# 8x8 diagonal blocks inverted by forward substitution on VectorE in a hybrid decoder trunk

## What is computed

```
    m = jnp.where(strict, jnp.einsum('nbhcd,nbhsd->nbhcs', k_beta, k) * decay, 0.0)
    eye = jnp.eye(c, dtype=m.dtype)
    t_inv = lax.linalg.triangular_solve(eye + m, jnp.broadcast_to(eye, m.shape),
                                        left_side=True, lower=True)
    u = t_inv @ v_beta
    w = t_inv @ (k_beta * jnp.exp(gc)[..., None])
```

## Time and profile before

| | |
|---|---|
| time, median of 3 runs | 2122.13 us (2121.14 to 2122.16) |
| the profiled execution | 2121.77 us, its span 2119.9 us |
| TensorE (PE) busy | 2046.7 us, 97% of the span |
| VectorE (DVE) busy | 1084.8 us, 51% |
| ScalarE (ACT) busy | 756.4 us, 36% |
| GpSimd (POOL) busy | 737.0 us, 35% |
| mean granted TensorE clock | 0.99 |

### The profile page before, as it was taken

How to read it: one execution, slowest core, us unless ns; L and a number is a source line. 1 busy time by engine, 2 the same in 40 slices (tenths; PEclk the granted TensorE clock), 3 DMA queues, 4 the chain that set the end, 5 groups by cost and what they waited for, 6 DMA issues and landing times.

```text
span 2119.9 us, 34678 instructions
## 1 busy us (share of the span) xinstructions
PE 2046.7 (97%) x14608; PEld 1574.7 (74%) x14608; DVE 1084.8 (51%) x1782; ACT 756.4 (36%) x1180; POOL 737.0 (35%) x550
## 2 busy tenths in 40 slices
PE   5999999999999999999989999999999999999997
PEld 4788787756667888888867877876566678888886
DVE  6694654796843422222367844458967343222223
ACT  4541613344353432322253243133443434332322
POOL 2430303331313444444435122133222344444442
PEclk8999999999999999999999999999999999999998
DMA  5320111221322323333332111122113223232331
GB/s 188 102 81 15 48 32 61 92 85 38 114 61 70 115 93 99 91 98 96 93 110 86 47 36 56 33 74 95 50 40 125 65 80 100 90 99 95 95 96 63
DMA packets 52266, 170.04 MB, mean 80 GB/s; under 512 B 5648, under 2 KB 13968, under 8 KB 51600
## 3 DMA queue, kind: packets, MB, share of 16 engines
q1 hardware_dynamic: 50928, 162.75, 24.1%
q0 software_dynamic: 1184, 5.07, 0.6%
HBM read 160.45 MB, written 7.34 MB: 79 GB/s over the span
## 4 chain that ended last, share of the span: by engine, by line
PE 84%; DVE 11%; ACT 3%; issue 1%; DMA 1%; SPq 0%; DVEq 0%; ACTq 0%
PE bank_a L467 13%; PE bank_a L468 12%; PE bank_a L471 12%; PE bank_v L471 7%; PE bank_v L467 7%; PE bank_v L468 7%; PE bank_v L609 5%; PE bank_v L531 4%; DVE mg L1425 1%; DVE arena L1419 1%; PE bank_a L739 1%; PE bank_f L563 1%; PE bank_f L569 1%; PE bank_f L542 1%; PE bank_a L728 1%
## 5 line engine op out<-in xcount | busy, mean ns | idle before, releaser
L428 POOL TENSOR_TENSOR w_lo<-ring,w_hi 128x512 fp32r<-128x512 f32 x536 | 730.6, 1384 | 1263.2 <-ACT w_hi L1107 1263.1
L467 PE MATMUL bank_a<-h_hi,w_hi 128*128 128x512 f32 x1312 | 531.0, 405 | 6.7 <-ACT w_hi L1107 6.7
L468 PE MATMUL bank_a<-h_lo,w_hi 128*128 128x512 f32 x1312 | 512.7, 391 | 0.0
L1107 ACT ACTIVATE w_hi<-ring 128x1024 fp32r<-128x1024 f32 x268 | 281.6, 1051 | 222.4 <-DVE arena L1951 220.1
L471 PE MATMUL bank_a<-h_hi,w_lo 128*128 128x512 f32 x1312 | 324.1, 389 | 0.0
L467 PEld LDWEIGHTS bank_a<-h_hi,w_hi 128*128 128x128 f32 x1312 | 247.2, 188 | 77.7 <-issue 19.4
L468 PEld LDWEIGHTS bank_a<-h_lo,w_hi 128*128 128x128 f32 x1312 | 247.3, 188 | 58.3 <-issue 8.1
L471 PEld LDWEIGHTS bank_a<-h_hi,w_lo 128*128 128x128 f32 x1312 | 246.3, 188 | 51.2
L467 PE MATMUL bank_v<-parts,w_hi 128*128 128x512 f32 x640 | 254.5, 398 | 1.4 <-DVE parts L1922 1.4
L468 PE MATMUL bank_v<-parts,w_hi 128*128 128x512 f32 x640 | 253.4, 396 | 0.0
L1419 DVE TENSOR_TENSOR sg<-bank_v,sg 128x512 f32<-128x512 f32 x112 | 77.5, 692 | 327.3 <-PE bank_v L471 256.3
(11 more groups left out here) (281 smaller groups left out, 2430.2 us busy)
## 6 DMA issues: line engine op xcount, KB each, us to landing
ring<-in_w SPq DMA_DIRECT2D x268, 512.0 KB, 3.5
out_ring<-in_w SPq DMA_DIRECT2D x64, 128.0 KB, 3.5
x_dram<-arena SPq DMA_DIRECT2D x2, 2048.0 KB, 8.9
arena<-x_dram SPq DMA_DIRECT2D x2, 2048.0 KB, 9.8
arena<-in_x SPq DMA_DIRECT2D x2, 1024.0 KB, 8.1
arena<-tabs POOLq DMA_DIRECT2D x4, 512.0 KB, 4.5
out_x<-arena SPq DMA_DIRECT2D x2, 1024.0 KB, 4.3
par<-in_par POOLq DMA_DIRECT2D x2, 937.0 KB, 7.1
```

The source lines that it names most:

```text
L428: ins = nc.gpsimd.tensor_tensor(w_lo[:, g % SPLIT, ks, :], raw, w_hi[:, g % SPLIT, ks, :].bitcast(F32), ALU.subtract)
L467: mm(b[:], w_hi[:, s, k, :], hi[:, k, :], start=k == 0, stop=False)
L468: mm(b[:], w_hi[:, s, k, :], lo[:, k, :], start=False, stop=False)
L1107: act_fn(w_hi[:, g % SPLIT, :, :], ring[:, g % RING, :, :], ACT.Copy).then_inc(S["split_hi"], 1)
```

## The change

The three smallest block sizes are taken out of the doubling: `first_steps` (block size 2) and the levels 2 and 4 go, and the 8x8 diagonal blocks are inverted directly.

- `block_columns` on VectorE: `u` is multiplied by a mask of the 8x8 blocks (128x1024), and a reduction over the block index packs the eight columns of each row's block into a compact tile `uc` of 128x128 (16 pairs by 8).
- `spread_rows` on TensorE: seven matmuls against 0/1 matrices `row0` to `row6` (128x128, in `consts`) copy row k of each block to all eight rows of the block, for columns k+1 to 7. They go into one bank of `bank_v`, in the middle of the gate product (after its 16 matmuls with `w_hi`, ahead of the 8 with `w_lo`).
- `block_inverses` on VectorE: a copy of the identity, and for k = 0 to 6 a product of the spread row with column k of the inverse, and a subtraction from the later columns. Every operation waits for the one before. Two operations of 128x512 put the compact inverse back into the 64x64 layout.
- `block_columns` stands between `masked` for `u` and the next `masked`; `block_inverses` stands where `first_steps` stood.
- `consts` loses four tiles of 64 columns and gains one of 64, one of 8 and seven of 128.

```diff
-LEVELS = (2, 4, 8, 16, 32)
+LEVELS = (8, 16, 32)
+BLOCK = 8
...
-    parts.append(("first_c", half(-1.0 * level(1).T)))
+    parts.append(("blocks_c", half(i // BLOCK == j // BLOCK)))
+    parts.append(("eye_b", (i % BLOCK == j)[:, :BLOCK]))
+    for k in range(BLOCK - 1):
+        parts.append((f"row{k}", i == j // BLOCK * BLOCK + k))
...
-        ("eye_c", half(np.eye(P))),
...
-            def split_product(g, b, hi, lo, sem_name=None, k0=0):
+            def split_product(g, b, hi, lo, sem_name=None, k0=0, between=None):
...
+                if between:
+                    between()
                 pe.wait_ge(S["split_lo"], g + 1)
...
+            def spread_rows(l, x, V):
+
+                b, reader, emptied = banks.next("v", x + "_e")
+                pe.wait_ge(reader, emptied)
+                pe.wait_ge(S[x + "_uc"], at(l, x + "_uc", 1))
+                uc, at_ = compact(V, 0), 0
+                for k in range(BLOCK - 1):
+                    n = M * (BLOCK - 1 - k)
+                    ins = mm(b[:, at_:at_ + n], cst(f"row{k}"), uc[:, :, k + 1:BLOCK], start=True, stop=True)
+                    at_ += n
+                ins.then_inc(v_full, 1)
...
-                numbers = [gate(l, 2, 0)]
+                numbers = [gate(l, 2, 0, lambda: spread_rows(l, "r", R))]
...
-                numbers.append(gate(l, 2, 7))
+                numbers.append(gate(l, 2, 7, lambda: spread_rows(l, "g", G)))
...
-            def first_steps(x, V):
+            def block_columns(x, V):
+
+                tt(V["x"], V["u"], cst("blocks_c").unsqueeze(1).to_broadcast([P, M, C]), MUL)
+                v.tensor_reduce(compact(V, 0), V["x"].rearrange("p m (b j) -> p m j b", j=BLOCK), AX_X, ADD).then_inc(S[x + "_uc"], 1)
+
+            def block_inverses(x, V):
+
+                xc = compact(V, 1)
+                link(v.tensor_copy(xc, cst("eye_b").unsqueeze(1).to_broadcast([P, M, BLOCK])))
+                dve.wait_ge(v_full, filled.next())
+                b, at_ = filled.bank(), 0
+                for k in range(BLOCK - 1):
+                    n = BLOCK - 1 - k
+                    product = compact(V, 2)[:, :, 0:n]
+                    ins = v.tensor_tensor(product, b[:, at_:at_ + M * n].rearrange("p (m c) -> p m c", c=n),
+                                          xc[:, :, k:k + 1].to_broadcast([P, M, n]), MUL)
+                    if k == BLOCK - 2:
+                        ins.then_inc(S[x + "_e"], 1)
+                        dve.wait_ge(S[x + "_e"], reached(x + "_e"))
+                    else:
+                        link(ins)
+                    tt(xc[:, :, k + 1:BLOCK], xc[:, :, k + 1:BLOCK], product, SUB)
+                    at_ += M * n
                 for half in range(2):
                     ms = slice(half * M // 2, (half + 1) * M // 2)
-                    tt(V["x"][:, ms, :], V["u"][:, ms, :], wide("first_c"), MUL)
-                    v.tensor_tensor(V["x"][:, ms, :], V["x"][:, ms, :], wide("eye_c"), ADD).then_inc(S[x + "_x1"], 1)
+                    shape = [P, M // 2, C // BLOCK, BLOCK]
+                    v.tensor_tensor(V["x"][:, ms, :].rearrange("p m (b j) -> p m b j", j=BLOCK), xc[:, ms, :].unsqueeze(2).to_broadcast(shape),
+                                    cst("blocks_c").rearrange("p (b j) -> p b j", j=BLOCK).unsqueeze(1).to_broadcast(shape), MUL).then_inc(S[x + "_x1"], 1)
...
                 masked("r", R["u"], lambda hp: wide("before_c"))
                 dve.wait_ge(S["r_tok"], at(l, "r_tok", 8))
+                block_columns("r", R)
                 masked("r", R["akk"], lambda hp: wide("before_c"))
-                first_steps("r", R)
+                block_inverses("r", R)
                 masked("r", R["ark"], lambda hp: wide("upto_c"))
                 masked("r", R["arb"], lambda hp: wide("upto_c"))
...
                 masked("g", G["u"], lambda hp: of_parity(G["d"], hp))
+                block_columns("g", G)
                 masked("g", G["arb"], lambda hp: of_parity(G["d"], hp))
-                first_steps("g", G)
+                block_inverses("g", G)
```

More of the change, by code:

```diff
@@ L41 @@
 RW_ORDER = (6, 7, 2, 3, 0, 1, 4, 5)
-LEVELS = (2, 4, 8, 16, 32)
-INVERSE_STEPS = ("x1", "ti", "y", "t", "x", "wt", "u")
+LEVELS = (8, 16, 32)
+BLOCK = 8
+INVERSE_STEPS = ("uc", "e", "x1", "ti", "y", "t", "x", "wt", "u")
 GDN0, MLA0, RWK0, DSA0, GATE0 = 0, 1032, 1448, 2472, 3824
@@ L260, in build @@
             ("r_ex", 1), ("r_sq", 1), ("r_l2", 2), ("r_l2s", 1), ("r_bsq", 2), ("r_bon", 2), ("r_feat", 4),
-            ("r_tok", 8), ("r_mat", 8), ("r_x1", 2), ("r_ti", 2), ("r_y", 10), ("r_t", 8), ("r_x", 10),
+            ("r_tok", 8), ("r_mat", 8), ("r_uc", 1), ("r_e", 1), ("r_x1", 2), ("r_ti", 2), ("r_y", 6), ("r_t", 4), ("r_x", 6),
             ("r_wt", 2), ("r_y1", 2), ("r_u", 2), ("r_ws", 2 * NC), ("r_s", NC), ("r_o", NC),
@@ L266, in build @@
             ("g_row", 2), ("g_d", 2), ("g_prep", 1),
-            ("g_tok", 6), ("g_mat", 4), ("g_x1", 2), ("g_ti", 2), ("g_y", 10), ("g_t", 8), ("g_x", 10),
+            ("g_tok", 6), ("g_mat", 4), ("g_uc", 1), ("g_e", 1), ("g_x1", 2), ("g_ti", 2), ("g_y", 6), ("g_t", 4), ("g_x", 6),
             ("g_wt", 2), ("g_u", 2), ("g_ws", 2 * NC), ("g_s", NC), ("g_o", NC),
@@ L317, in bank, with compact @@
                 return self.banks[(self.n - 1) % len(self.banks)]
+        def compact(V, i):
+            n = M * BLOCK
+            return V["y"].rearrange("p m c -> p (m c)")[:, i * n:(i + 1) * n].rearrange("p (m c) -> p m c", c=BLOCK)
         def of_parity(view, hp):
@@ L504, in token_root, with gate @@
                 ins.then_inc(v_full, 1)
-            def gate(l, br, m):
+            def gate(l, br, m, between=None):
                 g = begin_unit(("merge", br, m), l)
@@ L510, in gate @@
                 pe.wait_ge(reader, emptied)
-                split_product(g, b, h_hi, h_lo).then_inc(a_full, 1)
+                split_product(g, b, h_hi, h_lo, between=between).then_inc(a_full, 1)
                 return merges_to(g)
```

## The result

The changed kernel takes 2084.73 us (median of 4 runs, 2081.71 to 2086.87) where the kernel before takes 2122.05 beside it: a ratio of 0.9823, 95% interval [0.9808, 0.9838].

A forecast was written before the change was run, and what follows sets the result against it. TensorE, busy 97% of the span, was taken as the bound, with VectorE late ahead of RWKV's levels. 2 x (6.2 - 11.35 + 1.6 - 11.44) + 1.0 = -29.0 us gave 2093, range 2085 to 2102.

The forecast's parts named there:

- Levels: Two full levels go from each inversion: 11.35 us of TensorE in RWKV, 11.44 in GDN, all on the path.
- RWKV delay: The first `y` left in the RWKV branch comes 6.2 us later, VectorE being late; bounds 3.5 to 9.3.
- The chain: Seven dependent products and seven subtractions on VectorE in `block_inverses`: 3.64 us with gaps.
- the spreading: Seven matmuls on TensorE that spread the rows, 0.23 us each whatever the width: 1.6 us in all.
- the reduction: VectorE's reduction of 1024 elements that makes `uc`: 1.22 us, with the gap 1.26.
- POOL's hits: POOL's pair delays RWKV's last subtraction and two 128x512 operations, all with both inputs in SBUF: two hits, 2.0 us.
- GDN delay: 1.6 us from the seven matmuls; VectorE's 4.0 us slack just used up, a dearer chain or reduction adding the rest.
- Start: Constants grow by 712 columns, 365 KB, ahead of the weight tiles in SP's queue: 1.0 us, once.
- Rival 1: TensorE's clock falls around its RWKV stall: 5 us lost in two layers, 2098, or 2103 if worse; chance 0.18.
- a sign of being wrong: Clock column at 0.50 behind the stall, levels not at 5.7 us, or VectorE's added work above 8 us an inversion.
- Rival 2: A weight tile or table is late for the earlier scan; half of the 45.6 us lost, 2115; chance 0.03.
- Rival 3: VectorE pays for short runs in chain and reduction; at 1.0 us per chain operation 41 us more, 2134; chance 0.02.

The follow-up runs named there:

- the version with 32 bytes more: The changed kernel with 32 unused bytes per partition, so `parts` starts at 32 modulo 128 instead of 0: 2096.85 us, ratio 0.9883 to the kernel before.
- the additions: The changed kernel with the reduction in `block_columns` replaced by three halving additions: 2079.81 us, ratio 0.9806 to the kernel before.
- the permuted product: The changed kernel with the masked product written permuted, in two halves, so the reduction reads adjacent elements: 2084.78 us, ratio 0.9831 to the kernel before.

## Why the prediction was off, point by point

- **The step that failed** is the sum's silence on everything outside the inversions and the start. It counted what the change adds and removes, and read the 712 more columns only as 365 KB on a queue. They also shift every tile behind them, and `parts` came to a start of 0 modulo 128, which is worth 12.3 us in busy time and 13.0 in the kernel before by itself. None of the rivals held it. It could have been suspected: before, the same 128x512 matmul took 391 ns on `h_lo` and 396 on `parts`, a difference that nothing in the code explains.
- **Levels** (-11.35, -11.44): right; 44.7 us for all against 45.6.
- **RWKV delay** (6.2): from first mask to last `y` 7.3 in layer 0 and 6.4 in layer 1 (11.35 less the gains of 4.06 and 4.91). The chain (3.64 against 3.65) and the spreading (1.71 against 1.6) were right. Three sizes were off: the reduction (1.98, not 1.22), POOL's hits (none, where 2.0 was counted) and TensorE, which was late by 1.00 and had a hole of 1.27 in layer 0. The forecast said that TensorE would not be the later one; that held only while its clock did.
- **GDN delay** (1.6): 2.2 and 2.4 (11.44 less 9.21 and 9.05), from the reduction, whose overrun had no cover left. The prediction named this case.
- **Start** (1.0): 0.80 at the norm, and gone by the first mask; in other executions of kernels with these constants up to 1.9.
- **Rival 1, the clock**: the mechanism came, in both layers, to 0.68 and 0.70, and to the 0.50 that the prediction named as a sign of being wrong in the version with 32 bytes more. The price of 5 us did not: in the profiled executions, what it cost on TensorE it about gave back by moving POOL's pair. It was priced alone, where it should have been priced with what the delayed gate moves.
- **Rival 2**: nothing was given back later. **Rival 3**: chain operations took 0.19 to 0.28 us, on runs of 7 to 1 elements. Short runs cost nothing to be seen; strides did, in the reduction.

So 29.0 forecast, 24.8 measured for the change without the shift, and 12 to 13 us from the shift. The range failed on a term that it had no place for, and the errors inside the sum went the other way.

## To carry to other kernels

A change in the size of a constant or a buffer moves all tiles behind it: compare the mean duration of the untouched groups first, and test with a few unused bytes before the gain is put down to the edit. Work that one engine must wait for costs more than the stall when it lowers TensorE's clock behind it, and what a delay moves (here POOL's pair) can pay it back or double it, so an edit that removes one of the two alone may show nothing. Before a strided operand is written, weigh it against a few dense additions.

## What the runs showed of the hardware

- A 128x512 matmul of `wo` and `down` took 389 ns as a mean with its moving operand's tile at a start of 0 modulo 128 bytes, 391 at 64, 395 to 396 at 32 and 96 (second and third groups). In a full row of them, 38.77 against 39.88 us for 173. The weights and the output kept their place; whether theirs matter too was not tried, nor why 64 lies between.
- VectorE's 128x1024 reduction took 1.98 to 2.08 us at a stride of 8 elements and 1.22 when adjacent; a product written at a stride of 8 took 1.10 for 128x512 instead of 0.69.
- A COPY from SBUF was also held up under a POOL instruction (0.79 instead of 0.23), while operations with one input in PSUM were not (0.28, 2.87). The Trainium skill, in "SBUF — State Buffer" under "SBUF: two separate sides", counts both two SBUF inputs and VectorE's two-port modes as users of the shared ports; the rows agree, if this copy runs in such a mode, which no trace shows.
- The hole in RWKV's first level of layer 0 (no releaser shown) was 1.27 us in the changed kernel and with the additions, 0.98 with the permuted product, 0.44 with 32 bytes more, and nothing where TensorE's stall ahead of the spread rows was filled or shortened. But the kernel without the levels 2 and 4, which spreads no rows, has one of 0.34 in its first level too. Its cause is open.
